# A hybrid encoder trunk on one core: the gated mixer's head roots in two halves, and the last mixer batch turned at another place

## The reference, cut to what matters

```python
for l in range(DEPTH):
    h = rms_norm(x, norm_mix_g[l])
    proj = h @ w_in[l]
    q, k, v, z_b, x_c = jnp.split(proj, splits, axis=-1)
    mix_a = neighbourhood_attention(q, k, v, rpb[l])   # 8 heads, 512 channels
    mix_b = spatial_gating(z_b, ...)                   # 4 heads, 256 channels
    mix_c = fourier_mix(x_c)                           # 4 groups, 256 channels
    mix = head_rms_norm(jnp.concatenate([mix_a, mix_b, mix_c], axis=-1), head_norm_g[l])
    x = x + mix @ w_out[l]
    h = rms_norm(x, norm_ffn_g[l])
    x = x + (silu(h @ w_gate[l]) * (h @ w_up[l])) @ w_down[l]
return rms_norm(x, final_norm_g)

def head_rms_norm(y, g):   # per token and head of 64 channels
    yf = yf * lax.rsqrt(jnp.mean(yf * yf, axis=-1, keepdims=True) + EPS)
```

## Time and profile before

| what | us |
|---|---|
| median of 3 runs | 2003.94 (2003.3 to 2004.91) |
| the profiled execution, its own time | 2003.47 |
| its span in the profile | 2001.7 |
| PE busy | 1981.2 (99% of the span) |
| DVE busy | 1526.0 (76%) |
| ACT busy | 892.2 (45%) |
| POOL busy | 220.7 (11%) |

### The profile page before, as it was taken

The page is one execution under the profiler, slowest core; times in us unless marked ns, Lnnn a source line. Parts: engine busy times, 40 slices in busy tenths (PEclk is TensorE's granted clock), DMA queues, the critical chain, the costliest instruction groups (busy, mean ns, idle before and its releaser), DMA issues.

```text
span 2001.7 us, 28816 instructions
## 1 busy us (share of the span) xinstructions
PE 1981.2 (99%) x10528; PEld 1648.0 (82%) x10528; DVE 1526.0 (76%) x2511; ACT 892.2 (45%) x1611; POOL 220.7 (11%) x156
## 2 busy tenths in 40 slices
PE   8999999999999999999999999999999999999998
PEld 8887788888888888888898878888888888888887
DVE  8847874798777777787777488567997777778877
ACT  7453873443333333444544549535333333344443
POOL 1221453100000000000013123530000000000000
PEclk9999999999999999999999999999999999999999
DMA  7865843124332338533478668431443233293333
GB/s 248 214 168 152 233 159 116 43 102 172 132 106 95 105 108 293 170 96 95 121 218 195 156 159 246 137 105 58 136 159 111 94 106 107 99 346 96 96 99 122
DMA packets 130988, 288.91 MB, mean 144 GB/s; under 512 B 12960, under 2 KB 17952, under 8 KB 130592
## 3 DMA queue, kind: packets, MB, share of 16 engines
q1 hardware_dynamic: 107584, 241.97, 37.1%
q0 software_dynamic: 10880, 20.97, 6.2%
q10 hardware_dynamic: 12384, 24.12, 3.3%
HBM read 227.77 MB, written 59.24 MB: 143 GB/s over the span
## 4 chain that ended last, share of the span: by engine, by line
PE 91%; DVE 5%; issue 2%; ACT 1%; POOL 1%; DMA 0%; DVEq 0%; SPq 0%; ACTq 0%; POOLq 0%
PE bank L2245 27%; PE bank L2247 27%; PE bank L2246 27%; PE bank L2466 2%; PE bank L2394 1%; PE bank L2544 1%; DVE s_lo L1484 1%; POOL head_rstd L868 1%; DVE t_lo L1909 0%; PE bank L2481 0%; PE bank L2488 0%; PE bank L2357 0%; ACT h_hi L919 0%; PE bank L2373 0%; ACT s_hi L992 0%
## 5 line engine op out<-in xcount | busy, mean ns | idle before, releaser
L2245 PE MATMUL bank<-t_hi,s_hi 128*128 128x512 f32 (+1 forms) x1336 | 516.9, 387 | 0.8 <-DVE hid_cu L2022 0.5
L2247 PE MATMUL bank<-t_hi,s_lo 128*128 128x512 f32 (+1 forms) x1336 | 516.3, 386 | 0.0
L2246 PE MATMUL bank<-t_lo,s_hi 128*128 128x512 f32 (+1 forms) x1336 | 516.3, 386 | 0.0
L2245 PEld LDWEIGHTS bank<-t_hi,s_hi 128*128 128x128 f32 x1336 | 250.9, 188 | 52.5 <-DVE hid_cu L2022 1.3
L2246 PEld LDWEIGHTS bank<-t_lo,s_hi 128*128 128x128 f32 x1336 | 250.9, 188 | 50.8
L2247 PEld LDWEIGHTS bank<-t_hi,s_lo 128*128 128x128 f32 x1336 | 250.9, 188 | 50.7
L2245 PE MATMUL bank<-b_hi,s_hi 128*128 128x512 f32 x528 | 206.0, 390 | 0.1
L2247 PE MATMUL bank<-b_hi,s_lo 128*128 128x512 f32 x528 | 205.5, 389 | 0.0
L2246 PE MATMUL bank<-b_lo,s_hi 128*128 128x512 f32 x528 | 205.4, 389 | 0.0
L992 ACT ACTIVATE s_hi<-w_u 128x512 fp32r<-128x512 f32 x142 | 89.7, 632 | 232.9 <-PE bank L2247 175.4
L992 ACT ACTIVATE s_hi<-w_down 128x512 fp32r<-128x512 f32 x154 | 97.3, 632 | 200.4 <-PE bank L2247 199.6
(11 more groups left out here) (296 smaller groups left out, 3702.6 us busy)
## 6 DMA issues: line engine op xcount, KB each, us to landing
w_raw<-in_win SPq DMA_DIRECT2D x51, 512.0 KB, 5.7
w_g<-in_wg SPq DMA_DIRECT2D x44, 512.0 KB, 3.6
w_u<-in_wu SPq DMA_DIRECT2D x44, 512.0 KB, 4.4
t_raw<-hidden_t SPq DMA_DIRECT2D x88, 256.0 KB, 2.6
w_raw<-in_win POOLq DMA_DIRECT2D x40, 512.0 KB, 6.5
t_raw<-hidden_b SPq DMA_DIRECT2D x66, 256.0 KB, 2.6
hidden_b<-hid_g SPq DMA_DIRECT2D x60, 256.0 KB, 2.0
hidden_t<-hid_x SPq DMA_DIRECT2D x44, 256.0 KB, 2.0
```

The costliest lines, as they stand in the source:

```text
L2245: nc.tensor.matmul(bank, lh, rh, start=start, stop=False, skip_group_check=reopened)
L2246: nc.tensor.matmul(bank, lh, rl, start=False, stop=False, skip_group_check=reopened)
L2247: return nc.tensor.matmul(bank, ll, rh, start=False, stop=stop, skip_group_check=reopened)
```

## The change

POOL takes the power of minus one half of MB's mean squares in two instructions of 128 x 16 columns in place of one of 128 x 32: first heads 0 and 1 of every block, then their product, then heads 2 and 3 and their product. Each product waits for its own root. The semaphore `hs_rstd` so counts three in a layer and not two, and the waits on it follow.

On PE `turn_batch(7)` moves from behind `turn_halves(5)`, where it stood in front of `scores(7)`, to between `values(5)` and `turn_halves(6)`. On ACT `batch_hi(7)` moves from directly behind `batch_hi(6)` to behind `probs(15)`. DVE's order is not changed.

```diff
                 pool.wait_ge(hs_var, l * 2 + 2)
-                nc.gpsimd.tensor_tensor(SR[:, :], SS[:, :], NHALF[:, :], ALU.pow).then_inc(hs_rstd, 1)
-                pool.wait_ge(hs_rstd, l * 2 + 2)
+
+                def heads_of(t, f):
+                    return t[:, :].rearrange("p (n h) -> p n h", h=4)[:, :, 2 * f:2 * f + 2]
+
                 for f in range(2):
+                    nc.gpsimd.tensor_tensor(heads_of(SR, f), heads_of(SS, f), heads_of(NHALF, f), ALU.pow)\
+                        .then_inc(hs_rstd, 1)
+                    pool.wait_ge(hs_rstd, l * 3 + 2 + f)
                     v = MB[:, :, f * P:(f + 1) * P].rearrange("p n (h d) -> p n h d", d=DH)
                     r = SR[:, :].rearrange("p (n h a) -> p n h a", h=4, a=1)[:, :, 2 * f:2 * f + 2]
                     nc.gpsimd.tensor_tensor(v, v, r.to_broadcast([P, 8, 2, DH]), ALU.mult).then_inc(hs_norm, 1)
...
-                    for n in {0: (), 6: (6, 7), 7: ()}.get(i, (i,)):
+                    for n in ((i,) if i else ()):
                         batch_hi(n)
...
                     if n:
-                        dve.wait_ge(hs_rstd, l * 2 + n)
+                        dve.wait_ge(hs_rstd, l * 3 + n)
...
-                    dve.wait_ge(hs_rstd, l * 2 + n + 1)
+                    dve.wait_ge(hs_rstd, l * 3 + n + 1)
...
                         values(i - 2)
                         if i in (2, 4, 5):
                             turn_batch(i + 1)
+                        elif i == 7:
+                            turn_batch(7)
                         turn_halves(i - 1)
-                        if i in (3, 6):
+                        if i == 3:
                             turn_batch(i + 1)
```

## The result

The changed kernel takes 2007.82 us (median of 19 runs, 2007.46 to 2010.3), the kernel before 2003.75 (19 runs). The ratio is 1.0021, with a 95% interval of 1.0015 to 1.0027: 4.1 us more. The forecast was 2007.2 in a range of 2004.6 to 2008.8. The profiled execution has a span of 2005.8 us against 2001.7.

A forecast was written before the change was run, and what follows sets the result against it. PE, 99% busy, was taken to bound the kernel, with POOL setting scores(5). Each layer loses 1.22 + 0.44 = 1.66 us, two lose 3.3: median 2003.94 + 3.3 = 2007.2 us, range 2004.6 to 2008.8.

The forecast's parts named there:

- PE already waited for POOL at scores(5): Before the change, POOL's first query remainder, done at 215.46, was read as setting the start of scores(5) at 215.61.
- The unmarked gap of 0.31 us: PE late at scores(5): 0.66 us behind the turned halves' start, against 0.35 said to be one pair earlier.
- POOL's line gets 0.44 us longer: Two 16-column roots for one of 32 delay POOL's queued second product and query remainders, moving scores(5) to 216.05.
- the straight line: POOL root time through the 8- and 32-column sizes: 0.37 us per instruction plus 0.159 a column, 2.91 for 16.
- A half far from 2.9: Sign of being wrong in the profile after: a 16-column root on POOL not near 2.9 us.
- the bounds, 0.06 to 1.16: Limits on POOL's added time in us, with a half root at 2.72 or at 3.27.
- x stays to the end of the single pairs: x, POOL's added 0.44 us, passes undiminished behind scores(5) through the interlocked engines, along ACT's chain.
- Logits 16 are 1.22 us late through ACT's place: ACT's high part of batch 7 behind probs(15) delays DVE's low part and logits 16 queued behind it by 1.22 us.
- the likeliest case: Both delays cost, 1.66 us a layer, 3.3 in two; own range 2006.2 to 2008.7 us; chance 0.72.
- That the gaps close for a gain of 2.3 us: Rival: PE's two marked waits vanish and nothing replaces them, 1.16 us a layer, 2001.6 us; chance 0.07.
- the free moved batch: Rival: logits 16 have over 1.2 us in hand, only the second root costs, 2004.8 us; chance 0.13.
- The strided halves: Rival: each column of a POOL half root costs half as much again, 4.19 us a half, 2012.3 us; chance 0.05.

The follow-up runs named there:

- the kernel with both repairs: The changed kernel with pair 1's query low part on DVE and ACT's high part of batch 7 in its order of before; 2003.74 us, ratio 1.0002.

## Why the prediction was right, point by point

**PE already waited for POOL at scores(5).** Right, and shown: with the remainder on DVE the step takes 0.35 us. The unmarked gap of 0.31 us was the decisive row: it told that an earlier first product gives PE nothing. (The step of 0.35 that it was held against is that of scores(3), two pairs earlier and not one.)

**POOL's line gets 0.44 us longer.** Right in kind, too small: 0.92. The term that was mis-sized is the second root, put on the straight line like the first, at 2.91; it took 3.35, and the start of its product 0.08. The roots measured 2.93 + 3.35 + 0.08 - 5.45 = 0.91. What the sum left out, by the rows under "Why the second half takes 3.35 us", is DVE's query remainder, which the earlier product makes late and which then holds the second root. A half far from 2.9 was named as a sign of being wrong, and this half is 0.45 off. That the bounds, 0.06 to 1.16, held it was luck: the row they came from (two roots of 8 columns) has nothing to do with the reason.

**x stays to the end of the single pairs.** Right: logits 16 are 0.90 late with the halves alone.

**Logits 16 are 1.22 us late through ACT's place.** Right: 1.23 with the moved batch alone, and gone when ACT's order is put back. DVE's idleness was to be about 1.1 and was 1.29, PE's in front of the turned heads 1.08 and was 1.02.

**Sum.** 2 x (0.92 + 1.23) = 4.3 us by the measured terms, 4.1 measured, 3.3 forecast. The result lies in the upper half of the likeliest case, a hair over the 0.2% that had a chance of 0.22.

**The rivals.** That the gaps close for a gain of 2.3 us is out; so is the free moved batch. The Trainium skill (Perfetto Trace Analysis, section Optimization Strategy) advises to find the gaps on the busiest engine and make what they wait for start sooner. The change did so, and the trace shows the limit of it: both gaps closed, and the kernel lost 4.1 us, since what comes late next was not asked. The strided halves are out as well: 5.81 us with gaps and 5.80 without. The Trainium skill (GPSIMD Engine Reference, section Performance pitfalls for Q7 kernels) asks for an inner step of at most 8 bytes, and here it is 4. The trace agrees with that letter.

**Not foreseen.** The first product, now at 207.86 to 209.77, meets DVE's query remainder:

```profile
208.93 1.39 DVE L1727 TENSOR_TENSOR q_lo<-q_raw,q_hi 128x512 fp32r<-128x512 f32 x1
```

That row is the changed kernel's timeline of DVE; the same instruction takes 0.69 us in the kernel before, under the root. It cost PE a wait for the next copy of 0.49 us in place of 0.24, hidden here by the wait for POOL behind it, and it is what the second root met.

## What to carry to other kernels

A wait that is taken away is worth only what the next late thing leaves of it; so look at the step behind it, also where the view marks no wait, and compare that step's length with its length elsewhere. Splitting an instruction to get its first result sooner makes the last one later: ask who is queued behind the last, and whom the earlier piece now meets on other engines. When a step moves on one engine, its followers on the others must move to where their own queues are idle, not to the matching place in the order.

## What the runs showed of the hardware

A POOL root (power of minus one half) took 1.64 us for 8 columns, 2.93 for 16 and 5.45 for 32, close to a straight line of 0.37 us and 0.159 for each column. Where DVE was in the middle of an instruction that reads two whole SBUF tiles, the root took 0.31 to 0.94 us more, nearly the rest of that instruction.

DVE's subtraction of two SBUF tiles takes 0.69 us alone and 1.39 where it starts while POOL multiplies; it then ended 0.55 us behind the product's end. The Trainium skill (GPSIMD Engine Reference, section Key points) says that POOL shares its SBUF interfaces with DVE and contends with DVE instructions that have two SBUF inputs. The trace agrees: a copy from a bank kept its 0.55 beside a product (at 212.04 in the kernel before). But a root of POOL that was already running did not slow the same subtraction (0.69 at 208.99 in the kernel before).

The load of the third band of v can come too late for PE. One execution of the kernel with both repairs took 2007.83 us where the median is 2003.74; its waits of PE, in total, times and longest, hold 2.6 of these 4.1 us:

```profile
PE bank L2471 <- DMA v_band<-v_scratch: 2.6, 2, 2.3
```

The profiles of the other kernels show 1.1 us of it in one (POOL's remainder on DVE) and none in most, so the medians probably hold executions with and without such a wait, and differences of half a microsecond between them are not to be trusted.
